# Late norm scaling ahead of the seven feed-forward layers of a three-block network, and low halves of weights moved between VectorE and GpSimd

## What is computed

```python
def rmsnorm(x, g):
    xf = x.astype(jnp.float32)
    y = xf * lax.rsqrt(jnp.mean(xf * xf, axis=-1, keepdims=True) + RMS_EPS)
    return (y * g.astype(jnp.float32)).astype(x.dtype)
...
def modulate(h, shift, scale):
    return h * (1 + scale[:, None, :]) + shift[:, None, :]
def swiglu(h, w13, w2):
    a, b = jnp.split(h @ w13, 2, axis=-1)
    return (jax.nn.silu(a) * b) @ w2
...
def conv_glu_ffn(h, w_up, conv_w, conv_b, w_down):
    z = h @ w_up
    z1 = shift_prev(z)
    z2 = shift_prev(z1)
    z = conv_w[0] * z2 + conv_w[1] * z1 + conv_w[2] * z + conv_b
    gate, val = jnp.split(z, 2, axis=-1)
    return (jax.nn.silu(gate) * val) @ w_down
```

## Time and profile before

| | |
|---|---|
| median of 3 runs | 2327.18 us (2322.79 to 2336.35) |
| the profiled execution's own time | 2330.64 us |
| span of its records | 2328.8 us |
| mean granted TensorE clock | 0.958 |
| PE, DVE, ACT, POOL busy | 96%, 62%, 50%, 22% of the span |
| HBM read | 434.75 MB, 188 GB/s over the span |

### The profile page before, as it was taken

One profiled execution on the slowest core, in us unless ns is written; L12 is line 12 of the kernel. 1 busy time (PEld: TensorE's weight loads), 2 busy tenths in 40 slices (PEclk: granted clock), 3 DMA queues, 4 the chain that ended last, 5 costly groups with the idle time before them and its releaser, 6 DMA issues.

```text
span 2328.8 us, 45915 instructions
## 1 busy us (share of the span) xinstructions
PE 2237.0 (96%) x18384; PEld 2152.7 (92%) x18384; DVE 1436.0 (62%) x1989; ACT 1165.8 (50%) x1587; POOL 508.9 (22%) x257
## 2 busy tenths in 40 slices
PE   8989999988999899999999999998999999999998
PEld 7869799988899899999899999997799989999998
DVE  4464279964689858986659963345642353557554
ACT  5511165645655544456554454455554455555554
POOL 0023000010000034532135534420035410001443
PEclk9889699999999999999899999999999999999999
DMA  6220158854278748764257855553255543444452
GB/s 250 98 46 1 37 217 316 305 185 163 82 281 306 270 143 332 312 271 166 89 211 307 341 187 203 189 187 145 83 189 180 198 165 145 145 169 160 180 195 93
DMA packets 63374, 439.07 MB, mean 189 GB/s; under 512 B 6887, under 2 KB 9480, under 8 KB 10778
## 3 DMA queue, kind: packets, MB, share of 16 engines
q1 hardware_dynamic: 59472, 430.75, 49.6%
q10 hardware_dynamic: 3786, 6.65, 1.2%
HBM read 434.75 MB, written 2.62 MB: 188 GB/s over the span
## 4 chain that ended last, share of the span: by engine, by line
PE 66%; DVE 18%; issue 9%; ACT 4%; POOL 1%; DMA 1%; DVEq 1%; SPq 0%; ACTq 0%; POOLq 0%
PE ps L283 15%; PE ps L284 15%; PE ps L285 15%; DVE mix L587 10%; DVE w_lo L268 3%; PE ps L400 1%; PE ps L411 1%; ACT w_hi L262 1%; PE ps L297 1%; PE ps L299 1%; PE ps L305 1%; PE ps L1402 1%; DVE gf L710 1%; DVE acc L698 1%; DMA mix<-in_modw 1%
## 5 line engine op out<-in xcount | busy, mean ns | idle before, releaser
L283 PE MATMUL ps<-h_hi,w_hi 128*128 128x256 f32 x3544 | 991.0, 280 | 7.0 <-DVE w_lo L268 3.7
L284 PE MATMUL ps<-h_lo,w_hi 128*128 128x256 f32 x3544 | 985.6, 278 | 0.0
L285 PE MATMUL ps<-h_hi,w_lo 128*128 128x256 f32 x3544 | 985.4, 278 | 0.0
L268 DVE TENSOR_TENSOR w_lo<-ring,w_hi 128x2048 fp32r<-128x2048 f32 x273 | 625.3, 2292 | 497.8 <-ACT w_hi L262 489.4
L262 ACT ACTIVATE w_hi<-ring 128x2048 fp32r<-128x2048 f32 x335 | 640.6, 1914 | 132.8 <-PE ps L285 126.5
L283 PEld LDWEIGHTS ps<-h_hi,w_hi 128*128 128x128 f32 x3544 | 669.2, 189 | 14.8 <-issue 9.3
L284 PEld LDWEIGHTS ps<-h_lo,w_hi 128*128 128x128 f32 x3544 | 671.1, 189 | 0.2
L285 PEld LDWEIGHTS ps<-h_hi,w_lo 128*128 128x128 f32 x3544 | 669.1, 189 | 0.0
L283 PE MATMUL ps<-g_hi,w_hi 128*128 (+1 forms) x1232 | 344.8, 280 | 16.2 <-DVE g_lo L720 12.8
L284 PE MATMUL ps<-g_lo,w_hi 128*128 (+1 forms) x1232 | 343.3, 279 | 0.0
L285 PE MATMUL ps<-g_hi,w_lo 128*128 (+1 forms) x1232 | 343.1, 279 | 0.0
(11 more groups left out here) (420 smaller groups left out, 2533.7 us busy)
## 6 DMA issues: line engine op xcount, KB each, us to landing
ring<-in_weights SPq DMA_DIRECT2D x335, 1024.0 KB, 4.8
mix<-in_modw SPq DMA_DIRECT2D x72, 1024.0 KB, 5.0
bias_rows<-below_mix ACTq DMA_DIRECT2D x1, 1536.0 KB
mix<-in_c_ssd ACTq DMA_DIRECT2D x1, 1536.0 KB, 7.8
x<-in_x SPq DMA_DIRECT2D x1, 1024.0 KB, 4.8
mix<-in_c SPq DMA_DIRECT2D x2, 512.0 KB, 5.6
mix<-bias_rows ACTq DMA_DIRECT2D x1, 1024.0 KB, 9.3
out_xT<-hf SPq DMA_DIRECT2D x1, 1024.0 KB, 4.2
```

The lines of the kernel that those rows point to most:

```text
L268: dve.tensor_tensor(w_lo[:, n % SLOTS], ring[:, n % SLOTS], w_hi[:, n % SLOTS], ALU.subtract).then_inc(lo_ready[n % SLOTS], 1)
L283: pe.matmul(o, w[0], a_hi, start=first, stop=False, **kw)
L284: pe.matmul(o, w[0], a_lo, start=False, stop=False, **kw)
L285: return pe.matmul(o, w[1], a_hi, start=False, stop=last, **kw)
```

## The change

All seven layers become "late". While the last down unit of the stage ahead is still running, ACT copies x times the norm's gain (without the root's factor) to s_hi and DVE subtracts to s_lo, and PE starts units b and b+1 on these. For layers with modulate the shift stands in two further columns, so these matmuls have 258 columns. PE's sums over channels stand behind unit b, and the broadcast of the factor inside unit b+1. DVE multiplies the factor into the two units' outputs (function scaled) before ACT and DVE go on with them. Units b+2 onward use h_hi and h_lo, which are made as before. The spare matmuls are gone there. fin1 is fused: its factor and ffn2's come from one pass of sums, and DVE rescales x in four steps inside ffn2 (late_dve_rescale).

The low halves change hands. Unit b: after a feed-forward layer POOL makes it (before: DVE, in halves between the residual's steps). Unit b+1: DVE whole behind s_lo (before: DVE in halves after a mixer, POOL after a feed-forward layer). Unit b+2: DVE, ahead of the root. Unit b+3: POOL (before DVE). Unit b+4, the fifth: DVE, behind h_lo and ahead of scaled.

```diff
+            s_hi = over.enter_context(nc.sbuf_tensor("s_hi", [P, KD, T + 2], F32R))
+            s_lo = over.enter_context(nc.sbuf_tensor("s_lo", [P, KD, T + 2], F32R))
...
+        LATE = ("ffn0", "ffn1", "ffn2", "ffn3", "ffn4", "ffn5", "ffn6")
+        FUSED = {"ffn2": "fin1"}
...
+        def late_out(tag, m, blk):
+
+            if shifted_at[tag] is not None:
+                return ps[2 + 2 * m + blk][:, 0:T + 2]
+            return ps[2 + m][:, blk * T:(blk + 1) * T]
...
+        def late_act_squares(act, tag, gain, ready):
+            if shifted_at[tag] is not None:
+                a = shifted_at[tag]
+                act.wait_ge(*after(f"dve:mod{a // 72}"))
+                act.activation(s_hi[:, :, T], mod[:, a:a + 8], ACT.Copy)
+                act.activation(s_hi[:, :, T + 1], mod[:, a:a + 8], ACT.Copy).then_inc(*step(f"act:{tag}.shift"))
+            for q, (k, n) in enumerate(square_tiles(tag, KD)):
+                act.wait_ge(*ready(q)[0])
+                for j in range(k, k + n):
+                    act.activation(s_hi[:, j, 0:T], x[:, j], ACT.Identity,
+                                   scale=gain(j)).then_inc(*step(f"act:{tag}.s{j}"))
+                act.activation(hf[:, k:k + n], x[:, k:k + n], ACT.Square).then_inc(*step(f"act:{tag}.sq{q}"))
+                if q == 0:
+                    act.activation(root[:, 2:3], eps_at[1e-6], ACT.Sqrt)
+        def late_act(act, tag, gain, shift, ready):
+            b = late_first(tag)
+            late_act_squares(act, tag, gain, ready)
+            hi(act, b + 2)
+            if tag in FUSED:
+                act.wait_ge(*after(f"dve:{tag}.var"))
+                act.activation(root[:, 0:2], fold[:, 2:4], ACT.Sqrt, scale=1.0 / D).then_inc(*step(f"act:{tag}.rms"))
+                act.activation(fold[:, 4:6], late_sums(tag, 0), ACT.Sqrt, scale=1.0 / D,
+                               bias=eps_at[1e-6]).then_inc(*step(f"act:{tag}.rms1"))
+            else:
+                norm_act_root(act, tag, D, 1e-6)
+            hi(act, b + 3)
+            norm_act_parts(act, tag, KD, shift)
+            act.activation(rstd[:], ps[7][:, 0:T], ACT.Copy).then_inc(*step(f"act:{tag}.over"))
+            hi(act, b + 4)
...
+        def late_pe(pe, tag):
+            b, cols, two_banks = late_first(tag), late_columns(tag), shifted_at[tag] is not None
+            s = b % SLOTS
+            pe.wait_ge(lo_ready[s], b // SLOTS + 1)
+            if two_banks:
+                pe.wait_ge(*after(f"dve:{stage_ahead(tag)}.res1"))
+            for k in range(KD):
+                pe.wait_ge(*after(f"act:{tag}.s{k}"))
+                for blk in range(2):
+                    c, o = (2 * k + blk) * P, late_out(tag, 0, blk)
+                    pe.matmul(o, w_hi[:, s, c:c + P], s_hi[:, k, 0:cols], start=k == 0 and (two_banks or blk == 0),
+                              stop=False, skip_group_check=True)
+                    pe.matmul(o, w_lo[:, s, c:c + P], s_hi[:, k, 0:cols], start=False, stop=False, skip_group_check=True)
+            for k in range(KD):
+                pe.wait_ge(*after(f"dve:{tag}.s{k}"))
+                for blk in range(2):
+                    c = (2 * k + blk) * P
+                    done = pe.matmul(late_out(tag, 0, blk), w_hi[:, s, c:c + P], s_lo[:, k, 0:cols], start=False,
+                                     stop=k == KD - 1 and (two_banks or blk == 1), skip_group_check=True)
+            done.then_inc(unit_done, 1)
+            if tag in FUSED:
+                for k in range(KD):
+                    if k % 2 == 0 or k == KD - 1:
+                        pe.wait_ge(*after(f"act:{tag}.sq{k // 2 + (k == KD - 1)}"))
+                    for c in range(NCH):
+                        done = pe.matmul(ps[0][:, 2 * c:2 * c + 2], hf[:, k, c * P:(c + 1) * P],
+                                         gains_sq[tag][:, 2 * k:2 * k + 2], start=k == 0 and c == 0,
+                                         stop=k == KD - 1 and c == 1, skip_group_check=True)
+            else:
+                for k, w in ((6, "act:{}.sq3"), (7, "act:{}.sq4"), (0, "pool:{}.sum")):
+                    pe.wait_ge(*after(w.format(tag)))
+                    for c in range(NCH):
+                        done = pe.matmul(ps[0][:, c:c + 1], hf[:, k, c * P:(c + 1) * P], ones[:, 0:1],
+                                         start=k == 6 and c == 0, stop=k == 0 and c == 1, skip_group_check=True)
+            done.then_inc(*step(f"pe:{tag}.ss"))
+            n, s = b + 1, (b + 1) % SLOTS
+            pe.wait_ge(lo_ready[s], n // SLOTS + 1)
+            for blk in range(2):
+                for k in range(KD):
+                    c = (2 * k + blk) * P
+                    done = product(pe, late_out(tag, 1, blk), (w_hi[:, s, c:c + P], w_lo[:, s, c:c + P]), s_hi[:, k, 0:cols],
+                                   s_lo[:, k, 0:cols], k == 0 and (two_banks or blk == 0),
+                                   k == KD - 1 and (two_banks or blk == 1), skip_group_check=True)
+                    if blk == 0 and k == 3:
+                        late_pe_over(pe, tag)
+            done.then_inc(unit_done, 1)
+        def late_pe_over(pe, tag):
+            pe.wait_ge(*after(f"dve:{tag}.rstd"))
+            for c in range(NCH):
+                done = pe.matmul(ps[7][:, c * P:(c + 1) * P], rtok[:, c:c + 1].broadcast_to([P, P]), ident,
+                                 start=c == 0, stop=c == 1 and tag not in FUSED, skip_group_check=True)
+            if tag in FUSED:
+                for c in range(NCH):
+                    done = pe.matmul(ps[7][:, T + c * P:T + (c + 1) * P], fold[:, 6 + c:7 + c].broadcast_to([P, P]), ident,
+                                     start=False, stop=c == 1, skip_group_check=True)
+            done.then_inc(*step(f"pe:{tag}.over"))
...
+        def late_dve_lows(dve, tag, gain, q):
...
+            for j in range(k, k + n):
+                dve.wait_ge(*after(f"act:{tag}.s{j}"))
+                dve.scalar_tensor_tensor(out=s_lo[:, j, 0:T], in0=x[:, j], scalar=gain(j), in1=s_hi[:, j, 0:T],
+                                         op0=ALU.mult, op1=ALU.subtract).then_inc(*step(f"dve:{tag}.s{j}"))
+        def late_dve(dve, tag, gain, shift):
+            b = late_first(tag)
+            lo(dve, b + 1)
+            lo(dve, b + 2)
+            if tag in FUSED:
+                dve.wait_ge(*after(f"pe:{tag}.ss"))
+                dve.tensor_scalar(fold[:, 0:2], late_sums(tag, 0), 1e-6, D * 1e-12, ALU.mult,
+                                  ALU.add).then_inc(*step(f"dve:{tag}.var1"))
+                dve.wait_ge(*after(f"dve:{tag}.var1"))
+                dve.tensor_tensor(fold[:, 2:4], late_sums(tag, 1), fold[:, 0:2], ALU.add).then_inc(*step(f"dve:{tag}.var"))
+                dve.wait_ge(*after(f"act:{tag}.rms1"))
+                dve.reciprocal(fold[:, 6:8], fold[:, 4:6])
+            norm_dve_root(dve, tag)
+            norm_dve_parts(dve, tag, x, KD, gain, shift)
+            lo(dve, b + 4)
+        def late_dve_rescale(dve, tag, j):
+            for k in (2 * j, 2 * j + 1):
+                done = dve.scalar_tensor_tensor(out=x[:, k], in0=x[:, k], scalar=V(fin_gain[tag], k), in1=ps[7][:, T:2 * T],
+                                                op0=ALU.mult, op1=ALU.mult)
+            if j == 3:
+                done.then_inc(*step(f"dve:{tag}.source"))
+        def late_pool(pool, tag):
+            b = late_first(tag)
+            if tag not in FUSED:
+                norm_pool(pool, tag)
+                pool.wait_ge(*after(f"pool:{tag}.pair1"))
+                pool.tensor_tensor(hf[:, 0], hf[:, 0], hf[:, 2], ALU.add).then_inc(*step(f"pool:{tag}.four"))
+                pool.wait_ge(*after(f"pool:{tag}.four"))
+                pool.tensor_tensor(hf[:, 0], hf[:, 0], hf[:, 4], ALU.add).then_inc(*step(f"pool:{tag}.sum"))
+            lo(pool, b + 3)
...
-        def residual_dve(dve, tag, last_unit, factor=None, between=None):
+        def residual_dve(dve, tag, last_unit, factor=None, between=None, lows=None):
             for q, (k, n) in enumerate(square_tiles(tag, KD)):
                 if q == 1 and between is not None:
                     lo_half(dve, between, 0)
+                if q > 1 and lows is not None:
+                    lows(q - 2)
                 far = tag.startswith("ffn")
                 dve.wait_ge(*(after(f"pe:{tag}.b{q}") if q < 3 + far else (unit_done, last_unit + 1)))
                 for b in range(k, k + n):
@@ -479,6 +651,9 @@
                     done = dve.tensor_tensor(x[:, k:k + 2], ps[2 + q][:].rearrange("p (a b) -> p a b", a=2),
                                              x[:, k:k + 2], ALU.add)
                 done.then_inc(*step(f"dve:{tag}.res{q}"))
+            if lows is not None:
+                lows(3)
+                lows(4)
...
-            return n if n < UNITS else None
+            return n if n < UNITS and not next_late(s) else None
...
+                if m < 2:
+                    return
+                if m >= 4:
```

(63 more changed lines are left out.)

80 lines of the change are left out of this document (64 added, 16 removed).

## The result

The changed kernel takes 2354.9 us (median of 5), the kernel before 2334.7 us measured beside it (5 runs): 1.0114 times, with a 95% interval of 1.0077 to 1.0152. It is slower, and 20 us above the forecast of 2335. Of these 20, 7.5 are the kernel before, whose median over 5 runs lies that much above the 2327.2 of the 3 that were shown; the difference of the two kernels is 20.2 us where 7.9 was forecast. Measured once more in a later session it was 1.0082 (1.0046 to 1.0118) times before. The profiled execution took 2361.8 us, with a span of 2360.0. All ratios, and the medians told as differences, leave out executions over 1.5% above the fastest of the same kernel: up to five of the kernel before in one session, and one of 3647 us in the last version.

What follows compares the result with a forecast made beforehand. TensorE, busy 96%, was taken as the bound, with ffn0 and ffn1 ending on DVE and ffn2 to ffn6 on PE. Layer terms summed to +7.9 us on the profiled 2330.6, 2338.5, or 2335 on the median; range 2312 to 2350.

Steps and rivals of the forecast that it cites:

- the work on PE: At layer starts, PE's four units of 5.46 us plus sums and broadcast reach down 0 at 23.7, ffn2 26.5, without waits.
- The sums: At each layer's start on PE, 6 sums of two records of 0.115 us: 1.4 us, in ffn2 16 sums, 3.7 us.
- The pauses ahead of down 0: In ffn0, ffn1 and ffn6, PE was to wait 2 to 4 us before the first down unit.
- The low half of b+7: In ffn0 and ffn1, DVE finishes it at t = 43.4 instead of 38.0, so the layer ends 5.4 us later.
- rival 3: In ffn0 and ffn1, DVE's idle time takes up the 5.4 us lag: sum -2.9, 2324 us, chance 0.15.
- GpSimd against g_lo at ffn1's end: POOL's low half for ffn2 comes first by 0.2 us, so DVE's last g_lo waits 4.4 us.
- rival 1: POOL and DVE seldom meet, or DVE comes first; ffn2 to ffn6 gaps nearly all won: -14.7, 2312 us, chance 0.22.
- the 2 us to be lost again behind down 0: In ffn2, 0.9 us at the first modulation products and 1.1 at the end reduce -8.2 to -6.2.
- the pauses to be won: PE's gaps at layer starts, from first sum to first product: some 41 us, with ffn0 and ffn1 as 5 each.
- Rival 2: Without spare matmuls, the clock falls after pauses; slow matmuls cost 2 us in each of seven layers: 2349 us, chance 0.23.

Runs made afterwards that it cites:

- the last version: The change in ffn2 to ffn5 alone, with one spare matmul and GpSimd's low half held at ffn1's end: 2318.4 us, 0.9955 times the kernel before.
- GpSimd held: Changed kernel, but at ffn1's end GpSimd makes ffn2's first low half only after VectorE's last g_lo: 1.0119 times the kernel before (4 runs).
- the held run: Changed kernel with GpSimd's low half for ffn2 waiting for VectorE's last g_lo of ffn1: 1.0119 times the kernel before.

## Why the prediction was wrong

**The step that failed** is in the work on PE: "four units, each 5.46", before and after, and behind it that "nothing but fewer units or fewer pauses can make that shorter". The 5.46 was ffn4's in one profile. It is not a constant of the kernel. It is one of two spacings, 0.1133 or 0.1178 us a matmul, that PE takes up at a layer's start and mostly keeps to its end, at a granted clock of 1.00. The same profile had the other one in ffn6, 5.65 us a unit, and I did not compare the layers. Its window of PE there, to be read beside the earlier trace rows, where 181 us hold 1592:

```profile
2135.00:2300.00 165.00, 165.00 (x1403) 1.00 0.50 178
```

The changed kernel gets the wide one (0.1178) in every changed layer where 258 columns are followed directly by the stream of 256: 17 of 17 in five profiles. The kernel before gets it in 5 of 15. One matmul of 256 more takes it away (4 of 4), and so does one spare matmul (8 of 8 in two profiles). The price is the difference of the changed kernel's lengths of ffn2 to ffn5 to those with one spare matmul, 193.2, 190.5, 191.9 and 189.7 against 187.7, 186.6, 186.4 and 183.7 us: 20.9 us. Before loses a third of about as much by chance, 7 us. That leaves 14 us as a difference of the two kernels, on top of the sum of +8: 22. In ffn6 it is the other way round: unchanged it ran at 5.65 in 6 of 10 profiles, changed in 1 of 9, with mean lengths of 190.2 and 191.8 us. That is +1.6 where the table below, with both at 5.44, has +5.0. So the estimate is some 19 us, where 20.2 was measured (the interval of the ratio is 18 to 35 us). Without the wide spacing in the changed layers the same estimate is -2 us, and with the spare matmul, which removes it, the ratio is 0.9988 (0.995 to 1.0027), -3 us.

**The terms of the sum**, from each layer's start to the next stage's, all at 5.44 us a unit (with the one spare matmul, against the profile of before; ffn6 against the second profile of before):

| | forecast | measured |
|---|---|---|
| ffn0 | +5.4 | 202.7 - 197.0 = +5.7 |
| ffn1 | +9.8 | 208.3 - 200.9 = +7.4 |
| ffn2 | -6.2 | 187.7 - 195.9 = -8.2 |
| ffn3 | -0.6 | 186.6 - 187.8 = -1.2 |
| ffn4 | -0.8 | 186.4 - 185.7 = +0.7 |
| ffn5 | -1.8 | 183.7 - 185.1 = -1.4 |
| ffn6 | +2.1 | 192.3 - 187.3 = +5.0 |
| sum | +7.9 | +8.0 |

The waits were forecast rightly in kind and mostly in size, but that the sum agrees to 0.1 us is luck: ffn1 and ffn2 lie 2.4 and 2.0 us under their terms, ffn6 and ffn4 2.9 and 1.5 above. Each length is that of one profile, and the same layer at the same spacing differs by up to 2 us between profiles (the changed ffn6 190.4 to 192.6). The parts:

- The sums took 1.39 us (1.4), down 0 of ffn0 came at t = 28.4 where 28.6 was forecast, and that of ffn6 at 28.6 (29.4). The pauses ahead of down 0 were 3.7, 3.1 and 3.5 us from matmul to matmul (2 to 4).
- The low half of b+7 was 5.0 us later than before (5.4). ffn0 did end that much later, so rival 3, in which the lag heals, is out. In ffn1 the lag came to less, +3.9 with GpSimd held (204.8 against 200.9) for a term of +5.4.
- GpSimd against g_lo at ffn1's end: POOL first by 0.2 us, g_lo of 4.62 us, and holding POOL back gave 3.9 us (4.4). It also answers rival 1, in which they seldom meet, as does the g_lo of up 1, done at t = 28.3 and not by 23.7. The Trainium skill's rule (SBUF — State Buffer, "Who interferes with whom") is that a VectorE instruction with two SBUF inputs contends with a GpSimd one that reads SBUF. By that rule the trace agrees: the g_lo, which has two, took 4.62 us beside POOL's 4.53. The modr of the held run has one SBUF input and took 4.55 us beside POOL's 4.58. The same section of the Trainium skill lists tensor_scalar, which modr is, among the instructions that can contend in a 2-port mode. Whether this one ran in such a mode no run here shows.
- ffn2 kept the whole 8.2; the 2 us to be lost again behind down 0 were not.
- Two sums in the working are off and bear on no term: the pauses to be won add up to 46 us with 5 each for ffn0 and ffn1, not 41, and rival 1 wins 4.2 in ffn5, where 27.4 against 23.7 is 3.7.

**Rival 2**, the clock, gave 2349, nearest to the result, but only a fraction of it was at work. The granted clock over the whole was 0.956 against 0.958, and 0.99 to 1.00 in the layers that lost the time. Behind the pauses ahead of down 0 it differs by layer, as the windows of PE there show (ffn6, ffn0, ffn1):

```profile
2186.00:2194.00 8.00, 7.87 (x44) 0.62 0.22 77
327.00:335.00 8.00, 8.00 (x56) 0.79 0.21 63
657.00:665.00 8.00, 7.84 (x69) 1.00 0.19 57
```

In ffn6 the unit ahead of down 0, with the pause, took 8.81 us and down 0 8.37, 2.8 more than the pause and two of 5.44. That is about what its term was too small by. In ffn0 it is 1.7 us, and in ffn1 nothing: some 4 us in all, not 14. And spare matmuls did not help by the clock, since the first units did not get shorter with four of them, and one, where nothing waited, did at least as much (0.9988 against 1.0031).

**Not settled.** What sets the spacing. The runs show that the last matmuls ahead of the stream decide it and that it repeats: in the changed kernel 256 gives the narrow spacing and 258 the wide one, in the kernel before six of 258 give the narrow and six of 256 the wide. So it is no property of the width alone. How the loads of weights fall between the matmuls is one candidate, which no run tries. Why it sometimes changes within a layer is open too.

## What to carry to other kernels

Before you forecast a kernel that TensorE bounds, count its matmuls per stretch in every stage and in more than one profile; if the spacing differs at the same granted clock, the change may move stages from one to the other, and 2 to 4% of a layer's time hung on it here. Then try one additional matmul, or another width, right ahead of the long stream: it costs 0.1 to 0.25 us a layer and was worth about 20 us over four layers here. Ask of each operation given to GpSimd what VectorE does in the 4.6 us after its release, not on average.
